# Two wide stores in place of six narrow ones for the rows of layer 0's experts

## The reference

```
def grouped_moe(h, w_router, router_bias, w_gate, w_up, w_down):
    ...                                   # two experts e_idx and two weights w for each token
    out = jnp.zeros_like(t)
    for e in range(N_EXPERTS):            # 16
        h_e = jax.nn.silu(t @ w_gate[e]) * (t @ w_up[e])      # D 1024 -> FF 512
        out = out + combine[:, e:e + 1] * (h_e @ w_down[e])   # FF 512 -> D 1024
    return out.reshape(shp)
```

## Time and profile before

| | us |
|---|---|
| median of 3 runs | 1466.73 |
| lowest and highest | 1465.39, 1467.75 |
| span of the profiled execution | 1467.6 |
| PE busy | 1403.9 (96%) |
| ACT busy | 527.6 (36%) |
| DVE busy | 695.9 (47%) |
| POOL busy | 157.1 (11%) |

### The profile page before, as it was taken

The page is one execution under the profiler, slowest core; times in us unless marked ns, Lnnn a source line. Parts: engine busy times, 40 slices in busy tenths (PEclk is TensorE's granted clock), DMA queues, the critical chain, the costliest instruction groups (busy, mean ns, idle before and its releaser), DMA issues. The chain is left out here.

```text
span 1467.6 us, 20788 instructions
## 1 busy us (share of the span) xinstructions
PE 1403.9 (96%) x8454; PEld 899.7 (61%) x8454; DVE 695.9 (47%) x1201; ACT 527.6 (36%) x955; POOL 157.1 (11%) x163
## 2 busy tenths in 40 slices
PE   4999999999999999999999979999998999999997
PEld 2787667646888864444444478876856997344433
DVE  3477986475834442100000035877675864223323
ACT  4554452357233341111111136544346453112112
POOL 0006970000000000000000030074000000000000
PEclk9999999999999999999999989999999999999999
DMA  9862104671131757999999592121577765999994
GB/s 355 250 153 92 53 6 172 229 287 59 58 115 58 286 203 290 374 389 396 402 397 411 226 330 83 58 72 44 200 258 289 284 232 230 387 427 428 427 427 167
DMA packets 102952, 352.37 MB, mean 240 GB/s; under 512 B 23104, under 2 KB 26304, under 8 KB 88000
## 3 DMA queue, kind: packets, MB, share of 16 engines
q1 hardware_dynamic: 99136, 338.09, 60.3%
q0 software_dynamic: 2976, 10.49, 2.1%
q10 hardware_dynamic: 736, 2.36, 0.4%
HBM read 341.48 MB, written 13.63 MB: 242 GB/s over the span
## 5 line engine op out<-in xcount | busy, mean ns | idle before, releaser
L1471 PE MATMUL bank<-narrow_slab,picked 128*64 128x512 f32 x256 | 114.7, 601 | 4.4 <-issue 4.2
L1202 PE MATMUL bank<-slab,feed 128*64 128x512 f32 x512 | 115.8, 605 | 0.2 <-issue 0.2
L1472 PE MATMUL bank<-narrow_slab,picked 128*64 128x512 f32 x256 | 114.7, 601 | 0.0
L864 PE MATMUL bank<-hT,ring 128*128 128x512 f32 (+1 forms) x256 | 102.8, 539 | 0.0
L3101 DVE TENSOR_TENSOR f_acts<-bank,f_silu 64x512 f32<-64x512 f32 x16 | 12.2, 764 | 188.8 <-ACT f_silu L2232 188.8
L1202 PEld LDWEIGHTS bank<-slab,feed 128*64 128x64 f32 x512 | 36.6, 139 | 71.9 <-issue 71.9
L1471 PEld LDWEIGHTS bank<-narrow_slab,picked 128*64 128x64 f32 x256 | 34.1, 138 | 70.2 <-issue 68.8
L2499 POOL DMA_INDIRECT feed_rows<-token_table,slot_token x16 | 14.6, 914 | 555.9 <-DVE slot_token L3033 346.4
L3280 DVE TENSOR_TENSOR hidden<-bank,gated 64x512 f32<-64x512 f32 x16 | 17.4, 1086 | 109.7 <-ACT gated L2374 109.7
L864 PEld LDWEIGHTS bank<-hT,ring 128*128 128x128 f32 x256 | 45.9, 191 | 32.0 <-issue 30.6
L1231 PE MATMUL bank<-slab,f_turned 128*64 128x512 f32 x256 | 58.5, 598 | 0.6 <-issue 0.6
(11 more groups left out here) (421 smaller groups left out, 3025.1 us busy)
## 6 DMA issues: line engine op xcount, KB each, us to landing
ring<-in_w_in SPq DMA_DIRECT2D x23, 2048.0 KB, 11.3
ring<-in_w_ada SPq DMA_DIRECT2D x16, 2048.0 KB, 11.1
slab<-in_w_gate SPq DMA_DIRECT2D x16, 2048.0 KB, 14.8
slab<-in_w_up SPq DMA_DIRECT2D x16, 2048.0 KB, 18.8
slab<-in_w_down SPq DMA_DIRECT2D x16, 2048.0 KB, 19.4
narrow_slab<-in_w_gate SPq DMA_DIRECT2D x16, 2048.0 KB, 15.5
narrow_slab<-in_w_up SPq DMA_DIRECT2D x15, 2048.0 KB, 20.9
narrow_slab<-in_w_down SPq DMA_DIRECT2D x15, 2048.0 KB, 24.6
```

What stands on the lines that cost most here:

```text
L864: mm = T.matmul(beside[0][:, a:TOK], w[:, k, c * P:(c + 1) * P], hT[:, k, a:TOK], start=(k == 0), stop=(k == KT - 1))
L1202: mm = T.matmul(bank[e % 2][NEAR * kind:NEAR * (kind + 1), :], feed[e % 2][:, k, 0:NEAR], w[kind][:, k, :], start=(k == 0), stop=(k == KT ...
L1471: T.matmul(bank[0][0:64, :], x, gate[:, k, :], start=(k == 0), stop=(k == KT - 1))
L1472: mm = T.matmul(bank[0][64:128, :], x, up[:, k, :], start=(k == 0), stop=(k == KT - 1))
```

## The change

The rows of an expert are stored by two transfers, each of all 128 partitions of `y_out`: the near part (512 columns) and the rest part (256 columns). To name where they go, the home of each is written with one more dimension in front: `s (c n) -> c s n`, with c = 2 for the near rows and c = 4 for the rest rows. `STORES` becomes 2. Of the last expert ACT issues the near transfer between its two copies, when the first one is done; SP issues the rest transfer behind the second.

```
-STORES = 6
+STORES = 2
...
-            return [near[:, c * 512:(c + 1) * 512] for c in range(2)], [rest[:, c * SEG:(c + 1) * SEG] for c in range(4)]
+            return near.rearrange("s (c n) -> c s n", c=2), rest.rearrange("s (c n) -> c s n", c=4)
+
+        def y_parts(e):
+
+            near, rest = y_out[e % 2][:, 0:512], y_out[e % 2][:, 512:512 + SEG]
+            return near, rest
...
                 def store_y(e):
                     sp.wait_ge(sem["y_kept"], 2 * e + 2)
-                    near, rest = y_homes(e)
-                    for half in range(2):
-                        sp.dma_start(near[half], y_out[e % 2][NEAR * half:NEAR * (half + 1), 0:512]).then_inc(sem[f"y_stored{e % 2}"], 16)
-                    for c in range(4):
-                        sp.dma_start(rest[c], y_out[e % 2][REST * c:REST * (c + 1), 512:512 + SEG]).then_inc(sem[f"y_stored{e % 2}"], 16)
+                    for home, part in zip(y_homes(e), y_parts(e)):
+                        sp.dma_start(home, part).then_inc(sem[f"y_stored{e % 2}"], 16)
...
                     sp.wait_ge(sem["y_kept"], 2 * N_EXPERTS)
-                    _, rest = y_homes(N_EXPERTS - 1)
-                    for c in range(4):
-                        sp.dma_start(rest[c], y_out[1][REST * c:REST * (c + 1), 512:512 + SEG]).then_inc(sem["y_stored1"], 16)
+                    sp.dma_start(y_homes(N_EXPERTS - 1)[1], y_parts(N_EXPERTS - 1)[1]).then_inc(sem["y_stored1"], 16)
...
                         S.activation(y_out[e % 2][:, 0:512], bank[6][:, :], ACT.Copy).then_inc(sem["y_kept"], 1)
+                        if e == N_EXPERTS - 1:
+                            act.wait_ge(sem["y_kept"], 2 * e + 1)
+                            act.dma_start(y_homes(e)[0], y_parts(e)[0]).then_inc(sem["y_stored1"], 16)
...
-                    act.wait_ge(sem["y_kept"], 2 * N_EXPERTS)
-                    near, _ = y_homes(N_EXPERTS - 1)
-                    for half in range(2):
-                        act.dma_start(near[half], y_out[1][NEAR * half:NEAR * (half + 1), 0:512]).then_inc(sem["y_stored1"], 16)
```

## The result

The changed kernel takes 1529.98 us (median of 5 runs, 1528.89 to 1532.36) against 1467.13 before (median of 5): a ratio of 1.0434, 95% interval 1.0422 to 1.0445. The profiled execution has a span of 1530.6 us.

What follows compares the result with a forecast made beforehand. PE bounds the kernel by a hair, with DMA slack used up; 1467.6 + 58 (loop) + 11 (hand-over) = 1536.6 us profiled, so a median of 1536 us, range 1518 to 1570.

Steps and rivals of the forecast that it cites:

- PE and the DMA both full, PE by a hair: In the loop: PE needs 17.4 us per expert, a mean DMA engine 16.7, the slowest about 17.9; slack used up.
- Outermost size sets the shares: In the stores: destination's outermost size 2 or 4 puts near rows on two engines, rest rows on four, overlapping.
- Rival 1: Stores stay even over 16 engines: loop unchanged, hand-over gains 1.6 us, 1465 us; chance 0.13, of which 0.03 for faster.
- 22.5 to 23.7 us per expert: Loop cadence on an engine carrying both stores: 6.8 us of stores beside 15.7 (mean engine) or 16.9 (slowest).
- rival 3: Near and rest engines don't overlap, near ones mean: 5.4 us per store, loop +34, hand-over +6, 1507 us; chance 0.06.
- Near product of expert 15 at +51 to +66, middle +58: End of loop: its up slab lands at 870.5 to 885.7, so PE starts there, not at 819.98.
- Hand-over +11: After the loop: POOL waits for every store, 39.6 us after expert 15's up slab lands, where it was 28.4.
- Layer 1 gets nothing back: After the hand-over: layer 1 starts later and regains nothing, for its first weights lie in the same ring.
- The price of a row: Store rows pass an engine at 24.2 GB/s: 6.8 us per expert for 163,840 B, bounds 6.1 and 11.4.
- The clock costs nothing: In the loop: a lower PE clock after idling loses 1.7 us, which fits in the 5 us PE waits per expert.
- the ring never runs dry: In the loop: gate and up of e+2 are issued with 16 us or more of other work still queued.
- The slabs' landing: In the loop: slabs would take 30 us or more to land.

Runs made afterwards that it cites:

- The even wide kernel: The change's two 128-partition stores, each written to a block that is one run of 128 rows (128x512, 128x256): 1465.95 us against 1466.74 for the kernel before.
- the narrow ones with 2, 4 and 8 shares: Kernel before with six stores, near stores' 64 destination rows written as 2x32, 4x16 or 8x8: 1517.93, 1486.82 and 1470.38 us.
- wide_last_only: Kernel before with six narrow stores for experts 0 to 14, only the last expert's two wide as in the change: 1470.37 us, ratio 1.0032.

## Why the prediction was right

It said 1536 us and a loss of 69; it was 1530 and 63. Step by step:

- **PE and the DMA both full, PE by a hair.** Held. In even shares the loop keeps 17.4 us. That engines have almost no slack is what the runs with 4 and 8 shares show.
- **Outermost size sets the shares.** This was the choice without a row. The even wide kernel and the narrow ones with 2, 4 and 8 shares settle it from both sides, for the destination; no run made the source's outermost size small. They agree with the rule that the Trainium skill gives in DMA: Bandwidth & Descriptors, "Why a DMA increments its semaphore by 16 and not by 1". Rival 1 was sized right for the kernel that has even shares: its hand-over is 0.9 us shorter, where 1.6 was reckoned, and nothing of it shows in the time. Its remark that 8 shares would hardly slow the loop was too mild: that kernel lost 5 us.
- **22.5 to 23.7 us per expert.** Measured 22.6, the mean engine's value. Both sets fall on the same two engines, as the shares of 12.9, 7.1 and 5.6% show: without the overlap (rival 3) it would be 21.1.
- **Near product of expert 15 at +51 to +66, middle +58.** It came at 874.84, +54.9. The profiled execution entered the loop 1.9 us earlier than before's (626.66 and not 628.52 for expert 4), so the loop itself cost 56.7. The middle of 58 had given these two engines half of the slow engine's surplus. In the cadence they behaved like mean ones, for which the sum gives 870.5; it was 4 us more, from an issue 1.9 us earlier, and no run tells what took these 6 us.
- **Hand-over +11.** Measured 39.5 - 28.4 = 11.1.
- **Layer 1 gets nothing back.** From POOL's first gather to the end it is 616.3 us, and was 619.2. The ten kernels of the experiments have 615.4 to 618.4 there, all with layer 1's program unchanged (four of them work there on mixed rows, and it takes no longer), so the 2.9 us are most likely the profiled execution of before and no gain. With the 1.9 ahead of the loop and 1.3 in it they make up the 6 us between 69 and the 63 between the two spans. The changed kernel's profiled execution is also the slowest of its five (1532.36 us, median 1529.98), so a median one loses some 2 us less than its trace adds up to; where, no trace shows.
- **The price of a row.** In the full queue 6.8 us per store held, also at half the bytes (20.7 us measured, 20.5 reckoned). In wide_last_only, on queues nearly empty, it was 8.
- **The clock costs nothing.** True of the change, where after each near product of 8.78 us or more PE waits again before the next. So the 5.2 us per expert above 17.4 are 3.7 of waiting and 1.4 of slower near products; the prediction looked for 5 to 6 us of idle time, and left the clock out of this split. The condition named for it (no cover by a wait) came true in the kernels with small surpluses.
- **What was missing or wrong.** The prediction let SP issue at once and put all the waiting into the ring. In fact an issue is held, up to 20 us on SP and 28 on ACT. The time didn't need it, and that is in part luck: the hold falls on the slabs too, and most of the other 14 engines stand idle for up to 8 us of a round ("the ring never runs dry" is true of the two full engines only), but the two full ones stay busy. With ACT as issuer the same hold cost another 22 us. DMA share and GB/s in the loop were as foretold (0.82, 315). The slabs' landing was not: 15 to 24 us and not 30 (one took 28, with 16 us of hold in it), since the held issue comes later. POOL's first gather, at 914.31, came just ahead of the 915 to 925 foretold.

## What to carry to other kernels

A transfer's price is that of the fullest DMA engine, and here the share of the 16 that a store used hung on the outermost size of its destination: joining transfers by putting a dimension of 2 or 4 in front concentrated them. Ask of each transfer what the outermost size is in the built program, and compare bytes per engine, not bytes per core, with the time per round. When the mean DMA share and PE's busy share both fall, look for one full engine.

## What the runs showed of the hardware

- Two of 16 engines moved 47 to 57 GB/s, 24 to 28 each, with stores of 2 KB and 1 KB rows from SBUF to HBM.
- A store with a destination of 2x64x512, issued on ACT, kept 12.9% of 16 engines busy; with one of 4x32x256 from SP beside it, the two kept 12.7%. Two queues, the same two engines.
- Surplus and cadence, with the mean engine at 15.8 us without stores: 2 shares 21.9 us (21.5 reckoned), 4 shares 19.6 (18.8), rest rows on 4 engines 18.8 (17.9), 8 shares 18.1 (17.5). The 0.4 to 0.9 us over the reckoning are partly the lower clock after a wait (up to 1.7 us each time) where no wait follows, as with 4 shares and with the rest rows. With 8 shares the clock has no part (1.00 throughout, all near products 7.09 us). The rest may be engines that are slower than the mean, such as the slab landings of before show; which engines, and why, no run here tells.
- The issue of transfers was held on SP and on ACT, on either's own queue, when two or four engines had more to do than the others: 18 to 20 us in most rounds for the two stores of an expert, which took 1.0 us with even shares. It isn't tied to stores: once the 16 us fell on the gate slab behind them (797.81 us), and the hold was 5 to 6 us each for near and rest stores with 4 shares. What amount of queued work sets it off, no run here tells.
